# Four-layer fp32 block on one core: paired 64-row score products, a shorter prologue chain, and attention steps moved

## What is computed

```python
# block a, per layer
z = rms_norm(x, norm_mix) @ w_in                    # 1024 -> 4768
y_a = mla_mixer(...)     # 8 heads, 96 for q and k, 64 for v, causal softmax attention
y_b = hgrn2_mixer(...)   # 4 heads of 128, decays; a scan over the sequence
x = x + (sigmoid(g_a) * (y_a @ w_proj_a) + sigmoid(g_b) * (y_b @ w_proj_b)) @ w_out
x = x + (silu(h @ w_gate) * (h @ w_up)) @ w_down    # h = rms_norm(x, norm_ffn)

# block b, per layer
proj = rmsnorm(x, norm_mix_2) @ w_in_2              # 1024 -> 3344
q, k, v, z, xbc, dt = split(proj)    # q: 8 heads of 64; k, v: 2 heads of 64, 4 q heads share one
attn = dilated_attention(rotary(q) / 8, rotary(k), v)
xbc = silu(causal_depthwise_conv(xbc, conv_w, conv_b))
y = rmsnorm((ssd(xs, dt, ...) + d_skip * xs) * silu(z))     # 16 heads of 64
x = x + concat([attn, y]) @ w_out_2
x = x + swiglu(rmsnorm(x, norm_ffn_2))
```

## Time and profile before

| | us |
|---|---|
| median of 3 runs | 1488.94 |
| lowest, highest | 1487.82, 1489.52 |
| profiled execution, its own time | 1489.31 |
| span of the profiled execution | 1487.5 |
| TensorE busy | 1465.1 |
| VectorE busy | 932.3 |
| ScalarE busy | 804.5 |
| GpSimd busy | 77.9 |

### The profile page before, as it was taken

One profiled execution on the slowest core, in us unless ns is written; L12 is line 12 of the kernel. 1 busy time (PEld: TensorE's weight loads), 2 busy tenths in 40 slices (PEclk: granted clock), 3 DMA queues, 4 the chain that ended last, 5 costly groups with the idle time before them and its releaser, 6 DMA issues.

```text
span 1487.5 us, 19465 instructions
## 1 busy us (share of the span) xinstructions
PE 1465.1 (98%) x7541; PEld 1252.7 (84%) x7541; DVE 932.3 (63%) x1292; ACT 804.5 (54%) x1292; POOL 77.9 (5%) x86
## 2 busy tenths in 40 slices
PE   8999999999999999999999999999999999999998
PEld 8888888888888888888888989888888988888886
DVE  5698765565557877655555677655555577755553
ACT  6764455444467544544445786544445686644443
POOL 0112100000002220000000000000000000000000
PEclk9999999999999999999999999999999999999999
DMA  8643356756465435576664443566664343556551
GB/s 285 215 144 122 120 169 190 206 184 189 118 211 171 147 107 157 161 224 187 193 185 119 122 144 114 160 205 203 185 194 136 112 145 124 157 184 193 187 186 57
DMA packets 178699, 245.85 MB, mean 165 GB/s; under 512 B 18976, under 2 KB 130096, under 8 KB 178608
## 3 DMA queue, kind: packets, MB, share of 16 engines
q1 hardware_dynamic: 178416, 244.54, 53.1%
q10 hardware_dynamic: 192, 0.08, 0.0%
HBM read 243.52 MB, written 1.05 MB: 164 GB/s over the span
## 4 chain that ended last, share of the span: by engine, by line
PE 84%; DVE 8%; ACT 6%; issue 2%; DVEq 0%; ACTq 0%
PE acc L547 15%; PE acc L541 15%; PE acc L544 15%; PE misc L541 10%; PE misc L544 10%; PE misc L547 10%; DVE w_lo L1342 3%; PE misc L639 2%; ACT w_hi L954 2%; PE misc L736 1%; PE misc L865 1%; ACT arena L1021 1%; PE misc L805 1%; PE misc L664 1%; PE misc L688 1%
## 5 line engine op out<-in xcount | busy, mean ns | idle before, releaser
L1342 DVE TENSOR_TENSOR w_lo<-w_raw,w_hi 128x1024 fp32r<-128x1024 f32 (+3 forms) x472 | 560.2, 1198 | 330.9 <-ACT w_hi L954 329.1
L954 ACT ACTIVATE w_hi<-w_raw 128x1024 fp32r<-128x1024 f32 (+3 forms) x472 | 480.5, 1029 | 285.9 <-PE misc L547 164.1
L541 PE MATMUL acc<-w_hi,h_hi 128*128 128x512 f32 (+3 forms) x832 | 209.2, 374 | 0.2 <-ACT h_hi L993 0.2
L547 PE MATMUL acc<-w_hi,h_lo 128*128 128x512 f32 (+3 forms) x832 | 201.4, 365 | 1.4 <-DVE arena L1693 1.4
L544 PE MATMUL acc<-w_lo,h_hi 128*128 128x512 f32 (+3 forms) x832 | 201.3, 365 | 0.0
L541 PE MATMUL misc<-w_hi,h_hi 128*128 128x512 f32 x640 | 175.5, 396 | 0.0
L544 PE MATMUL misc<-w_lo,h_hi 128*128 128x512 f32 x640 | 171.5, 390 | 0.0
L547 PE MATMUL misc<-w_hi,h_lo 128*128 128x512 f32 x640 | 171.5, 390 | 0.0
L547 PEld LDWEIGHTS acc<-w_hi,h_lo 128*128 128x128 f32 x832 | 148.5, 189 | 23.3 <-DVE arena L1693 1.8
L544 PEld LDWEIGHTS acc<-w_lo,h_hi 128*128 128x128 f32 x832 | 148.4, 189 | 22.3 <-DVE w_lo L1342 0.3
L541 PEld LDWEIGHTS acc<-w_hi,h_hi 128*128 128x128 f32 x832 | 142.7, 189 | 22.1 <-issue 1.8
(11 more groups left out here) (200 smaller groups left out, 1285.3 us busy)
## 6 DMA issues: line engine op xcount, KB each, us to landing
w_raw<-in_w_in SPq DMA_DIRECT2D x92, 512.0 KB, 3.9
w_raw<-in_w_gate SPq DMA_DIRECT2D x176, 256.0 KB, 2.9
w_raw<-in_w_up SPq DMA_DIRECT2D x176, 256.0 KB, 3.1
w_raw<-in_w_down SPq DMA_DIRECT2D x88, 512.0 KB, 3.6
w_raw<-in_w_out SPq DMA_DIRECT2D x40, 512.0 KB, 3.6
w_raw<-in_w_in SPq DMA_DIRECT2D x32, 388.0 KB, 3.4
w_raw<-in_w_in SPq DMA_DIRECT2D x16, 336.0 KB, 4.2
w_raw<-in_w_proj_a SPq DMA_DIRECT2D x8, 512.0 KB, 3.8
```

Of the source, the lines that this page charges most:

```text
L541: pe.matmul(dst, st[0][:, k, t * P:(t + 1) * P], rhs, start=first, stop=False)
L547: return pe.matmul(dst, st[1][:, k, t * P:(t + 1) * P], rhs, start=False, stop=last)
L954: act.activation(w_hi[:, g % RING, 0:w], w_raw[:, g % RING, 0:w], ACT.Copy)\
L1342: dve.tensor_tensor(w_lo[:, g % RING, 0:w], w_raw[:, g % RING, 0:w], w_hi[:, g % RING, 0:w].bitcast(F32), ALU.subtract)\
```

## The change

1. Prologue: 16 products of zeros instead of 8. The gain row of the first norm has a DMA and a semaphore of its own, first in ScalarE's queue; the other two are turned later, behind nT1, into `acc3`. ScalarE loads its table with a dummy copy at the start, and its first weight split stands behind the first turned tile instead of ahead of it.
2. Block b, q and k: the heads are stored in pairs (head j and head j+4 side by side), so that one full 128-wide tile turns two heads; ten turned tiles instead of twenty. One head lies on partitions 0 to 63, the other on 64 to 127, and so do the two k heads. `paired_scores` writes two score groups at once into two banks, and changes between the row halves with every product.
3. Block b: PT, S, O, `row_max`, `softmax`, `weighed` stand in pairs; the channel steps and the product copies lie between the pairs. The next-to-last z0 slot moves ahead of the xsT steps; these go 0, 2, 1, 3 and their copies split no weights first. The reads of `cs` and of O on VectorE split no weights first.
4. Block a: `weighed` stands ahead of the split and the `level` of its round.
5. Boundary: the third residual piece is added ahead of the two low copies (nT0, nT1), the fourth between them; the low copies of nT2 and nT3 have no weight splits ahead of them.
6. The bank of a score group counts as free when its first read is done, not when the row maximum is.

```diff
@@ -170,8 +170,8 @@
         nT0 nT1 qkv0 nT2 nT3 qkv0 qkv1 qkv1 cvT0 cvT1 qkv2 qkv2 xd0 xd0 qkT0 qkT1 qkT2 qkT3 qkT4 xd0 S0 S1 xd0
-        xd1 PT0 S2 xd1 xT0 O0 PT1 S3 xd1 O1 PT2 S4 xd1 xd2 O2 PT3 S5 xd2 xT1 O3 PT4 xd2 xT2 O4 PT5 xd2 O5
-        xd3 attT0 attT1 xd3 xT3 xd3 xd3 z0 xT4 xT5 z0 cs z0 xsT0 xsT1 xsT2 xsT3 z0 cr0 z1 cb0 cb1 cr1
+        xd1 xd1 PT0 PT1 S2 S3 xT0 xd1 O0 O1 xd1 xd2 PT2 PT3 S4 S5 xd2 O2 O3 xT1 xd2 xT2 xd2 PT4 PT5 xd3 O4 O5
+        xd3 attT0 attT1 xT3 xd3 xd3 z0 xT4 xT5 z0 cs z0 z0 xsT0 xsT2 xsT1 xsT3 cr0 z1 cb0 cb1 cr1
@@ -244,9 +244,17 @@
+def first_head(block, g):
+    if g < 2:
+        return 4 * g
+    return (2 * g - 4) if block == 0 else (0, 4, 2, 6)[g - 2]
...
+    if name in [f"S{g}" for g in range(6)]:
+        return "dve", f"Sread{name[1:]}"
@@ -365,7 +373,7 @@
-        qkT = (carve(14336, 16, T), carve(10784, HB + HKV, T))
+        qkT = (carve(14336, 16, T), carve(10784, HB // 2 + 1, T))
...
@@ -548,12 +559,11 @@
             pe.wait_ge(zeroed, 1)
-            for _ in range(8):
+            for _ in range(16):
...
-            pe.wait_ge(lb_in, 48)
-            pe.wait_ge(rows_0, 1)
-            pe.transpose(misc[3][:, 0:P], rows[:, :], ident).then_inc(lb_T, 1)
+            pe.wait_ge(mix_in, 16)
+            pe.transpose(misc[3][:, 0:8], first[0:8, :], ident[0:8, 0:8]).then_inc(lb_T, 1)
@@ -561,6 +571,8 @@
                 g = BASE[layer] + s
+                if layer == LAYERS[0] and name == "mla1" and i == 0:
+                    pe.wait_ge(shifted, 1)
@@ -640,15 +652,28 @@
             def scores(layer, g):
-                block = layer[0]
-                d, group = (DQK, 1) if block == 0 else (DB, HB // HKV)
...
-                qk = qkT[block]
+                qk = qkT[0]
...
-                    mm = pe.matmul(b[:, i * keys:(i + 1) * keys], qk[0:d, hd, nq * P:(nq + 1) * P],
-                                   qk[0:d, HB + hd // group, 0:keys], start=True, stop=True)
+                    mm = pe.matmul(b[:, i * keys:(i + 1) * keys], qk[0:DQK, hd, nq * P:(nq + 1) * P],
+                                   qk[0:DQK, HB + hd, 0:keys], start=True, stop=True)
...
+            def paired_scores(layer, g):
...
+                banks = [bank_of(layer, f"S{g + half}") for half in range(2)]
+                n, nq, keys = (4, 0, P) if g == 0 else (2, 1, T)
+                last = []
+                for i in range(n):
+                    pair = first_head(1, g) + i
+                    for half in range(2):
+                        rows_ = slice(DB * half, DB * half + DB)
+                        mm = pe.matmul(banks[half][:, i * keys:(i + 1) * keys], qkT[1][rows_, pair, nq * P:(nq + 1) * P],
+                                       qkT[1][rows_, HB // 2, 0:keys], start=True, stop=True)
+                        last.append(mm)
+                last[-2].then_inc(*PE.mark(f"S{g}"))
+                last[-1].then_inc(*PE.mark(f"S{g + 1}"))
...
@@ -687,10 +713,16 @@
                     tr.then_inc(*PE.mark(name))
+                    if layer == LAYERS[0] and name == "nT1":
+                        pe.wait_ge(lb_in, 32)
+                        pe.transpose(acc[3][:, 0:24], first[0:24, :], ident[0:24, 0:24]).then_inc(lb_T, 1)
...
-                    scores(layer, i)
+                    if block == 0:
+                        scores(layer, i)
+                    elif i % 2 == 0:
+                        paired_scores(layer, i)
@@ -775,8 +807,7 @@
                         pe.wait_ge(*DV_.at(layer, "qk"))
-                    transposes(layer, name, [zqkv[:, t, hd * DB:hd * DB + DQK] for hd in (2 * i, 2 * i + 1)
-                                             for t in range(NT)], DQK)
+                    transposes(layer, name, [zqkv[:, t, P * i:P * i + P] for t in range(NT)])
@@ -980,7 +1011,7 @@
                 if layer == LAYERS[0] and kind == "nT":
-                    split_until(layer, (1, 1, 2, 3)[i])
+                    split_until(layer, i)
@@ -1009,7 +1040,7 @@
                 block = layer[0]
-                t, h0 = (0, 4 * g) if g < 2 else (1, 2 * g - 4)
+                t, h0 = int(g >= 2), first_head(block, g)
...
@@ -1208,7 +1243,8 @@
                     t, half = i // 2, i % 2
-                    b = wait_bank(layer, f"xsT{i}")
+                    act.wait_ge(*PE.at(layer, f"xsT{i}"))
+                    b = misc[ORD[1].turn[f"xsT{i}"] % 4]
...
@@ -1271,7 +1307,7 @@
                 conv_silu(1)
-                for i in range(4):
+                for i in (0, 2, 1, 3):
...
@@ -1372,9 +1408,9 @@
                 if layer == LAYERS[0] and kind == "nT":
-                    split_until(layer, (1, 1, 2, 3)[i])
+                    split_until(layer, i)
...
-                    split_until(layer, 3 if kind == "nT" and i < 2 else ORD[layer[0]].before["misc", name] + LOOK)
+                    split_until(layer, 3 if kind == "nT" else ORD[layer[0]].before["misc", name] + LOOK)
@@ -1416,9 +1452,10 @@
                 dve.reciprocal(small[:, 176 + c:176 + c + n], small[:, 160 + c:160 + c + n]).then_inc(*DV_.mark())
-                b = wait_bank(layer, f"O{g}")
+                dve.wait_ge(*PE.at(layer, f"O{g}"))
+                b = misc[ORD[block].turn[f"O{g}"] % 4]
...
-                t, h0 = (0, 4 * g) if g < 2 else (1, 2 * g - 4)
+                t, h0 = int(g >= 2), first_head(block, g)
...
@@ -1555,6 +1595,13 @@
                     norm_operand(layer, f"nT{i}")
+                    if layer == LAYERS[0] and i == 1:
+                        dve.wait_ge(lb_T, 2)
+                        dve.tensor_copy(gcol[:, 1, :], acc[3][:, 8:16]).then_inc(gcol_0, 1)
+                        link(dve.tensor_copy(lbw[:, 0:8], acc[3][:, 16:24]))
+                        link(dve.tensor_tensor(lbw[:, 8:12], lbw[:, 0:4], lbw[:, 4:8], ALU.max))
+                        link(dve.tensor_tensor(lbw[:, 0:4], lbw[:, 0:4], lbw[:, 8:12], ALU.subtract))
+                        dve.tensor_tensor(lbw[:, 4:8], lbw[:, 4:8], lbw[:, 8:12], ALU.subtract).then_inc(shifted, 1)
@@ -1615,11 +1662,11 @@
                 for i in range(8):
+                    if 2 <= i < 8:
+                        weighed(layer, i - 2)
...
-                    if 2 <= i < 8:
-                        weighed(layer, i - 2)
@@ -1732,20 +1779,20 @@
                 row_max(layer, 2)
+                row_max(layer, 3)
...
-                row_max(layer, 3)
+                weighed(layer, 1)
...
-                weighed(layer, 1)
...
+                row_max(layer, 5)
...
-                row_max(layer, 5)
...
+                convolve(2)
...
-                convolve(2)
@@ -1764,7 +1811,8 @@
                 convolve(4)
-                b = wait_bank(layer, "cs")
+                dve.wait_ge(*PE.at(layer, "cs"))
+                b = misc[ORD[1].turn["cs"] % 4]
@@ -1855,11 +1903,7 @@
-            dve.tensor_copy(gcol[:, :, :], misc[3][:, 8:24].rearrange("p (i k) -> p i k", i=2)).then_inc(gcol_0, 1)
-            link(dve.tensor_copy(lbw[:, 0:8], misc[3][:, 0:8]))
-            link(dve.tensor_tensor(lbw[:, 8:12], lbw[:, 0:4], lbw[:, 4:8], ALU.max))
-            link(dve.tensor_tensor(lbw[:, 0:4], lbw[:, 0:4], lbw[:, 8:12], ALU.subtract))
-            dve.tensor_tensor(lbw[:, 4:8], lbw[:, 4:8], lbw[:, 8:12], ALU.subtract).then_inc(shifted, 1)
+            dve.tensor_copy(gcol[:, 0, :], misc[3][:, 0:8]).then_inc(gcol_0, 1)
...
```

53 lines of the change are left out of this document (32 added, 21 removed).

## The result

The changed kernel takes 1470.57 us, the median of 4 runs (1469.74 to 1472.15), and the kernel before 1488.38 (4 runs, 1487.75 to 1489.52). The ratio is 0.9878, with a 95% interval of 0.9866 to 0.9889: 17.8 us less. The profiled execution of after took 1469.74 (span 1467.9), the one of before 1489.31 (span 1487.5); between these two, 19.6 us went, 1.8 more than between the medians.

What follows compares the result with a forecast made beforehand. TensorE, busy 98% of the span, was taken as the bound. Terms of 1.2 + 3.4 + 2.4 + 1.9 + 3.4 + 1.4 + 1.6 = 15.3 us gave a 1473.6 us median, range 1469 to 1479.5.

Steps and rivals of the forecast that it cites:

- O4: Block b, paired steps: O4's wait for the PT4 copy, 0.7 a layer, goes; saves 1.4 us (0 to 1.4).
- Prologue: Kernel start: first slot near 9.9 as before but faster, sixth slot 1.2 earlier, ScalarE late; saves 1.2 us.
- Block a: Level-2 product's wait for VectorE's read of O0 goes, 1.7 us twice; saves 3.4 us (2.6 to 3.4).
- Boundaries and q and k: Layer boundaries: earlier residuals save 2.4 us; block b: ten full turned tiles instead of twenty save 1.9 us.
- Scores: Block b score products: row halves side by side and fewer 64-row visits save 3.4 us (0.7 to 4.9).
- loads in a line: Block b, 128-column score products: weight loads stay one behind the other, 1.86 us for the pair, saving 0.12.
- Rival 1: Block b scores: halves don't run side by side, saving only 0.35 us a layer; 1476.3 us; chance 0.23.
- rival 4: Block b scores: every change between row halves drains the array, kernel slower, 1493 us at 0.5 a change; chance 0.02.
- xsT and y0: Block b: xsT stalls go, but ScalarE's late line makes a wait of about 1.5 before y0; saves 1.6 us.
- Rival 2: Block b: ScalarE isn't late at y0 and score weight loads overlap too; 1469.2 us; chance 0.1.
- Rival 3: Block b: ScalarE becomes the bound of the joined attention, 6 us lost; 1479.6 us; chance 0.08.
- Rival 5: Block a, pairs, xsT: removed waits come back through another releaser; 1480 us at the far end, chance 0.02 there.

Runs made afterwards that it cites:

- the h_hi edit: Kernel after with ScalarE's copies of the second half of x (h_hi) ahead of three weight splits at a layer's start, both blocks; 1470.11 us, one run.
- e9_one_half_and_twos: Kernel after with 128-column score pairs changing row halves after every two products and 256-column pairs on rows 0 to 63 only; 1476.80 us, one run.
- e1_halves_in_turn: Kernel after with each score pair running all products on rows 0 to 63, then all on rows 64 to 127; median 1471.06 us.
- e2_weighed_late: Kernel after with `weighed` put back behind the weight splits and level of its round, block a only; 1474.88 us in one run.
- e4_boundary_back: Kernel after with the layer boundary of before: old order of residuals and low copies, weight splits ahead of second-half low copies; 1473.91 us, one run.
- e6_decays_first: Kernel after with z0 copies, first decays, first exponents and M0 ahead of ScalarE's and VectorE's weight splits; median 1471.44 us.

## Why the prediction was right, point by point

The forecast was 1473.6, and 1470.57 lies within the range, 3.0 us below the forecast and just below its own range of 1471 to 1476. The mechanisms were at work as described, but for the order in which score products start and for what bounds the prologue behind its first slots. Sizes were off, mostly too low: the sum was short by 4.3 between the profiles and by 2.5 between the medians. Experiments bear on the scores, block a, the prologue, the boundaries and the wait at y0. The terms of q and k and of O4 are read from the two traces alone, and what the earlier release of a score bank (item 6 of the change) gives by itself was not measured.

- **Prologue**, 1.2 against 1.9 in these two executions and 1.35 on average. The zero products ended at 6.87, not at 7.5, and the first slot did not start "near 9.9, as before" but at 9.32. That ScalarE's own line of work would be late by the sixth slot was wrong: the sixth slot started 1.9 earlier, and then ScalarE stood for the weights of the seventh (1.89 us, until 20.63), where TensorE lost 0.6 us or more in four of the nine profiles. That the clock rises in the prologue is an inference from products that become twice as fast; the granted clock reads 1.00 throughout it.
- **Block a**, 3.4 against 4.2. The mechanism was right. The step that failed is the pricing of a wait by its recorded length: the group of 16 products took 3.67 us with the stall in its middle and 1.71 without, 1.96 and not 1.70, and 0.14 more was lost in the next round. The same holds for O4 (0.94, and 0.12 in the group behind it, where 0.71 was recorded). Together this is 1.5 of the 4.3 us that the sum was short.
- **Boundaries and q and k**, right to 0.2 each, with the 1.06 wait for h_hi where "about 1 us" was forecast.
- **Scores**, 3.4 against 5.5. That the halves run side by side is shown by the experiment with one half (1.93 against 1.07). The failed step is "loads in a line": 16 instructions with a weight load each took 1.09 us, where 1.86 was taken and the other bound was 1.2. The step "instructions start in order and two of one half exclude each other" was also wrong: with halves in turn it would have given 1.9 for the 256-column pair, and it was 1.07, with starts out of that order (last section). Rival 1 and rival 4 (a cost at every change of half) are out.
- **Weight loads on row tiles.** An instruction of 128 columns with its load took (1.09 - 0.18)/16 = 0.057 us on two halves, by the prediction's estimate of 0.18 for the visit; that is half of the 0.107 of full tiles. 2.8 us a layer were saved. The Trainium skill (TensorEngine Tiling (Array Packing), Key Properties) says that tiles load weights and multiply in parallel, by which the forecast would have been 2.4 a layer instead of 1.7: the trace agrees with it.
- **xsT and y0**, 1.6 against 0.9. The recorded wait at y0 is 1.35 where 1.5 was forecast, and the walk along ScalarE named its cause. What was missing is what follows such a wait: y1 was 0.2 late as well and the groups behind each were 0.1 slower, 1.93 in all. The durations of that walk add up to 10.4, not to the 10.2 that it used, with which the forecast wait would have been 1.7. Rival 2 had this wait absent; it stayed.
- **Rival 3** did not come: apart from 0.15 at xT0 there is no wait in the joined attention. **Rival 5** did not either: none of the removed waits came back at its place.
- Busy time fell by 11.7 and not by 5, idle time by 7.9 and not by 10. The score products and the turning of q and k alone took 7.6 less, where 5.3 was forecast, and what a stall costs beyond its recorded wait counts as busy time.

## What to carry to other kernels

Read what a stall costs from the start of the group to the start of a later one, not from the recorded wait alone; here it was 0.3 to 0.6 us more, and a recorded 0.26 cost 0.82. When a change takes background work away from ahead of a step, ask whether the engine was idle there: the work comes back later, on the chain, and here putting it back was worth 3.7 us, a fifth of what the whole change gave. Make such an edit only where the wait stands: the h_hi edit gained 1.16 in each layer of block b and lost 0.82 in a layer of block a that had no wait. Products with 64 rows were worth spreading over both row halves here, even where up to four instructions of one half stood ahead of the other's.

## What the runs showed of the hardware

A product waits less for its neighbours than its place in the order says: four instructions on rows 0 to 63 ahead of the first on rows 64 to 127 cost nothing measurable at 256 columns, eight at 128 columns 0.55 us. The starts of the single instructions show how. On one half, in e9_one_half_and_twos, they come 0.22 us apart. In the 256-column pairs of e1_halves_in_turn they come two by two from the first on (822.34 and 822.35, 822.66 and 822.67), although the first four in order lie on one half. So an instruction on the idle half starts ahead of ones that stand before it for the other. With eight in front, at 128 columns, five start alone, from 813.25 to 813.79, before the first pair (813.79 and 813.80), so this reach has an end.

The pause at y0 sometimes costs more than itself. Seven profiles have this wait of 1.35 us. In four of them, at five of their eight pauses, TensorE's granted clock was lower soon behind it, as here behind the first of the two in e2_weighed_late (us, TensorE's busy time and instructions, granted clock, DMA share, GB/s):

```profile
885.00:890.00 5.00, 5.00 (x21) 0.67 0.66 212
890.00:895.00 5.00, 5.00 (x34) 1.00 0.30 106
```

A part of such a stretch (884.9 to 888.2 here) has a granted clock of 0.50, that is 1.2 instead of 2.4 GHz. It began after TensorE had stood still for 1.35 us and worked again for 1.3 to 2.0, and it costs 1.3 us: in e4_boundary_back 7.98 us pass from y0 to the step behind y1, in after 6.69. In the five profiles without a pause at y0 or y1 it was not seen. Pauses of 1.7 us elsewhere, in block a of before and of e2_weighed_late and at y1 of e6_decays_first, had none behind them either. So that the pause brings it about is likely, but not shown, and what decides whether it comes stays open.

The zero products do not take the same time in each execution: 16 of them took 5.20 to 6.51 us, with everything behind them moved by as much, while the granted clock is given as 1.00 throughout. The moment at which products become twice as fast lies between the first and the last of them. And ScalarE's split for the seventh slot, which waits for its weights to land, started between 20.6 and 22.2 us in the profiles of these kernels, although the second slot had started anywhere from 11.7 to 14.2. Each of these moves a single execution by 1 us or so; that they make up the whole spread between executions of one kernel was not tested.
